# Thirty-two more tokens get their expert activations from gathered rows instead of the dense product

## The reference, cut to what matters

```python
s1, s2 = einsum(q1, keys1), einsum(q2, keys2)        # 8 heads x 128 keys each
v1, i1 = top_k(s1, 16); v2, i2 = top_k(s2, 16)
top_s, top_c = top_k(v1[..., :, None] + v2[..., None, :], 16)
expert = e1 * 128 + e2                                # 128 slots per token
g = softmax(top_s)
act = gelu(einsum('thkd,td->thk', u_tab[expert], h))
y = einsum('thk,thkd->td', g * act, v_tab[expert])
```

## Time and profile before

| | |
|---|---|
| median of 3 runs | 1529.41 us (1522.24 to 1529.96) |
| profiled execution | 1525.89 us, span 1524.1 us |
| PE busy | 1492.7 us (98%) |
| DVE busy | 1204.3 us (79%) |
| ACT busy | 703.4 us (46%) |
| POOL busy | 1021.8 us (67%) |
| moved by DMA | 439.99 MB, mean 289 GB/s |
| granted TensorE clock, mean | 0.992 |

### The profile page before, as it was taken

The page is one execution under the profiler, slowest core; times in us unless marked ns, Lnnn a source line. Parts: engine busy times, 40 slices in busy tenths (PEclk is TensorE's granted clock), DMA queues, the critical chain, the costliest instruction groups (busy, mean ns, idle before and its releaser), DMA issues.

```text
span 1524.1 us, 21845 instructions
## 1 busy us (share of the span) xinstructions
PE 1492.7 (98%) x7979; PEld 1253.3 (82%) x7979; DVE 1204.3 (79%) x1979; ACT 703.4 (46%) x1312; POOL 1021.8 (67%) x622
## 2 busy tenths in 40 slices
PE   7999999899999999999999999999999999999997
PEld 4345684488899999999999999988888888788885
DVE  6878833526799899998888880288999899999998
ACT  2034653342344433488888883433333333333343
POOL 2621002654378888776777875698888888889866
PEclk8999999999999999999999999999999999999999
DMA  9986137133178898889999997799999999999981
GB/s 364 338 242 100 26 103 284 43 123 111 45 268 323 312 334 306 298 294 374 361 376 362 384 352 295 262 375 346 374 388 379 383 387 381 375 382 370 368 288 69
DMA packets 216599, 439.99 MB, mean 289 GB/s; under 512 B 38180, under 2 KB 128804, under 8 KB 214572
## 3 DMA queue, kind: packets, MB, share of 16 engines
q1 hardware_dynamic: 178764, 303.49, 57.0%
q0 software_dynamic: 36864, 134.23, 23.8%
q10 hardware_dynamic: 864, 0.86, 0.2%
HBM read 380.72 MB, written 56.64 MB: 287 GB/s over the span
## 4 chain that ended last, share of the span: by engine, by line
PE 61%; DMA 9%; DVE 7%; issue 7%; POOL 4%; ACT 2%; SPq 2%; DVEq 0%; ACTq 0%
PE ps L1846 12%; PE ps L1848 11%; PE ps L1847 11%; DMA a_in<-act_scr 4%; DMA v_raw<-in_peer_v 4%; PE ps L1869 3%; PE ps L1871 3%; PE ps L1870 3%; POOL vl L1737 3%; DVE ps L1941 2%; PE ps L1515 2%; PE ps L1516 2%; PE ps L1517 2%; PE ps L1861 1%; PE ps L1862 1%
## 5 line engine op out<-in xcount | busy, mean ns | idle before, releaser
L1731 POOL TENSOR_TENSOR utl<-u_raw,uth 128x1024 fp32r<-128x1024 f32 x128 | 312.8, 2444 | 139.1 <-ACT uth L1750 120.8
L1846 PE MATMUL ps<-h2h,uth 128*128 128x384 f32 x1024 | 347.8, 340 | 2.2 <-POOL utl L1731 1.5
L1737 POOL TENSOR_TENSOR vl<-v_raw,vh 128x1024 fp32r<-128x1024 f32 x128 | 309.8, 2421 | 50.9 <-ACT vh L1750 48.9
L1848 PE MATMUL ps<-h2h,utl 128*128 128x384 f32 x1024 | 342.8, 335 | 0.0
L1847 PE MATMUL ps<-h2l,uth 128*128 128x384 f32 x1024 | 342.6, 335 | 0.0
L1869 PE MATMUL ps<-vh,wh 128*128 128x512 f32 x768 | 299.7, 390 | 0.8 <-DVE wl L2067 0.7
L1871 PE MATMUL ps<-vh,wl 128*128 128x512 f32 x768 | 299.2, 390 | 0.0
L1870 PE MATMUL ps<-vl,wh 128*128 128x512 f32 x768 | 299.1, 390 | 0.0
L2062 DVE TENSOR_TENSOR w_f<-a_in,g_in 128x384 f32<-128x384 f32 x128 | 213.8, 1671 | 94.6 <-DMA a_in<-act_scr 93.5
L1750 ACT ACTIVATE vh<-v_raw 128x1024 fp32r<-128x1024 f32 x128 | 135.4, 1058 | 194.7 <-DMA v_raw<-in_peer_v 163.5
L1846 PEld LDWEIGHTS ps<-h2h,uth 128*128 128x128 f32 x1024 | 192.4, 188 | 2.7 <-POOL utl L1731 1.8
(11 more groups left out here) (375 smaller groups left out, 2235.1 us busy)
## 6 DMA issues: line engine op xcount, KB each, us to landing
u_raw<-in_peer_uT SPq DMA_DIRECT2D x128, 512.0 KB, 7.0
v_raw<-in_peer_v SPq DMA_DIRECT2D x128, 512.0 KB, 9.3
act_scr<-acts SPq DMA_DIRECT2D x64, 384.0 KB, 4.7
g_scr<-stage SPq DMA_DIRECT2D x12, 2048.0 KB, 9.6
g_in<-g_scr SPq DMA_DIRECT2D x32, 768.0 KB, 8.7
a_in<-act_scr SPq DMA_DIRECT2D x64, 384.0 KB, 9.3
w_ada<-in_w_ada SPq DMA_DIRECT2D x10, 2048.0 KB, 15.8
w_q<-in_peer_w_query SPq DMA_DIRECT2D x8, 1024.0 KB, 6.4
```

Of the source, the lines that this page charges most:

```text
L1731: tt(k.utl[b % 3][:, :, :].rearrange(f3), k.u_raw[:, b % 4].rearrange(f3), k.uth[b % 3][:, :, :].bitcast(F32).rearrange(f3), ALU.subtract) ...
L1737: tt(k.vl[:, n % 4], k.v_raw[:, n % 4], k.vh[:, n % 4].bitcast(F32), ALU.subtract).then_inc(k.vl_done, 1)
L1846: mm(o, hi, k.h2h[:, kt, SP:T], start=(kt == 0), stop=False)
L1848: ins = mm(o, lo, k.h2h[:, kt, SP:T], start=False, stop=(kt == DK - 1))
```

## The change

The dense tile shrinks from 384 to 352 columns in the u stage: tokens 128 to 159 (SPX = 32) are left out of the activation product. Their activations are made from gathered u rows as for the special tile. As there are only 32 of them, the 128 partitions hold four groups (GX): group g has all 32 tokens and a quarter of the slots (SLX = 32). So 32 more gathers suffice, 160 u rows in all. Their h is made from `x1_scr` and two rows of `mod_scr` (six DMAs, two operations on POOL at block 3). The indices are spread to the groups, and the dot products collected, by four small DMAs each. The columns of `acts` of these tokens are filled with ones once; gate x activation goes into the one-hot weights instead (`special_weights`), scaled by each token's largest value, and ACT undoes the scale in `evacuate_g` for the first 8 groups. The one-hot blocks move from 57..113 to 63..118. Rows are issued and used at other places: the first behind block 16, and 12 u rows are used in v blocks 1 to 6.

```diff
-HOT_FROM, HOT_TO = 57, 113
+HOT_FROM, HOT_TO = 63, 118
+SPX = 32
+GX = P // SPX
+SLX = SLOTS // GX
+U_ROWS = SLX + SLOTS
+ONES_PAST = SP + SPX
@@ row_steps
-    for j in range(2 * SLOTS):
-        if j < 53:
-            at = 7 + 0.86 * j
-        elif j < 125:
-            at = 53 + (j - 53) * 0.777
-        elif j < SLOTS:
-            at = 109 + (j - 125) * 0.5
-        else:
-            at = NBLK + 1 + (j - SLOTS) * 0.875
+    for j in range(U_ROWS + SLOTS):
+        if j < 47:
+            at = max(16.9 + 0.755 * j, 10.7 + 0.93 * j)
+        elif j < 131:
+            at = 55.5 + (j - 47) * 0.72
+        elif j < U_ROWS:
+            at = 116 + (j - 131) * 0.65
+        else:
+            at = NBLK + 7 + (j - U_ROWS) * 0.78
@@ experts
-    SP_GELU, SP_WEIGH = 4, 6
+    SP_GELU, SP_WEIGH = 9, 11
+    INDICES_AT, GELX_AT = 15, 45
@@ sync
+        def load_special_rows():
+            sp.wait_ge(k.q_evac, k.items_all)
+            sp.wait_ge(k.s_x1out, 16 * TT)
+            for g in range(GX):
+                sp.dma_start(k.hx[g * SPX:(g + 1) * SPX, :], k.x1_scr[SP:SP + SPX, :]).then_inc(s_hx, 16)
+            for dst, row in ((k.ring[6], k.mod_scr[1, 0:2]), (k.ring[7], k.mod_scr[0, 2:4])):
+                row = row.rearrange("g n -> (g n)")
+                sp.dma_start(dst[:, :], bass.AP(row.tensor, row.offset, [[0, P], [1, D]])).then_inc(s_hx, 16)
+
+        def spread_indices():
+            sp.wait_ge(k.spx_done, 1)
+            for g in range(GX):
+                sp.dma_start(k.rowx_at[g * SPX:(g + 1) * SPX, :], k.spx_at[0:SPX, g * SLX:(g + 1) * SLX]).then_inc(s_spx, 16)
+
+        def spread_scales():
+            sp.wait_ge(k.spx_done, 2)
+            sp.dma_start(k.spx_scr, k.sx[0:SPX, 1:2]).then_inc(s_spx, 16)
+            sp.wait_ge(s_spx, 16 * (2 * GX + 1))
+            sp.dma_start(k.sbx[:, :], bass.AP(k.spx_scr.tensor, k.spx_scr.offset, [[0, P], [1, SPX]])).then_inc(s_spx, 16)
+
+        load_special_rows()
         for b in range(NBLK):
             if b + 4 < NBLK:
                 load_u(b + 4)
+            if b == INDICES_AT:
+                spread_indices()
+            elif b == GELX_AT + 1:
+                collect_activations()
+            elif b == HOT_FROM - 1:
+                spread_scales()
@@ gpsimd
+            if b == 3:
+                pool.wait_ge(s_hx, 16 * (GX + 2))
+                k.pool_steps.on(pool)(tt(k.hx[:, :], k.hx[:, :], k.ring[6][:, :], ALU.mult))
+                tt(k.hx[:, :], k.hx[:, :], k.ring[7][:, :], ALU.add).then_inc(k.hx_ready, 1)
@@ scalar
-            nc.scalar.activation(k.acts[:, b % 4], ps[:, 2 + b % 2, 0:TD], ACT.Gelu_apprx_tanh).then_inc(k.gelu_done, 1)
+            nc.scalar.activation(k.acts[:, b % 4, SPX:], ps[:, 2 + b % 2, 0:T - ONES_PAST], ACT.Gelu_apprx_tanh).then_inc(k.gelu_done, 1)
+
+        def finish_special():
+            act.wait_ge(k.row_used, SLX)
+            copy(y_sp, k.h_row[:, :]).then_inc(k.h_sp, 1)
+            nc.scalar.activation(k.dotsx[:, :], k.dotsx[:, :], ACT.Gelu_apprx_tanh).then_inc(k.gelx_done, 1)
@@ evacuate_g
+            if n < SPX // HOTS:
+                act.wait_ge(s_spx, 16 * (2 * GX + 2))
+                for j in range(HOTS):
+                    ins = nc.scalar.activation(k.stage[:, ch % 2, :, at + j], ps[:, 4 + n % 2, j * PKEYS:(j + 1) * PKEYS], ACT.Copy,
+                                               scale=k.sbx[:, HOTS * n + j:HOTS * n + j + 1])
+                ins.then_inc(k.g_evac, 1)
+                return
-        EXP_AT = {5: 0, 12: 1, 29: 2, 48: 3}
+        EXP_AT = {6: 0, 13: 1, 32: 2, 53: 3}
@@ tensor, activations
-                mm(o, hi, k.h2h[:, kt, SP:T], start=(kt == 0), stop=False)
-                mm(o, hi, k.h2l[:, kt, SP:T], start=False, stop=False)
-                ins = mm(o, lo, k.h2h[:, kt, SP:T], start=False, stop=(kt == DK - 1))
+                mm(o, hi, k.h2h[:, kt, ONES_PAST:T], start=(kt == 0), stop=False)
+                mm(o, hi, k.h2l[:, kt, ONES_PAST:T], start=False, stop=False)
+                ins = mm(o, lo, k.h2h[:, kt, ONES_PAST:T], start=False, stop=(kt == DK - 1))
@@ vector
-        routing(1, (3, 3))
-        for it, rows in ((2, (5, 5, 5, 2, 4, 4)), (3, (5, 5, 4, 2, 3, 3))):
+        routing(1, (0, 0))
+        special_indices()
+        for it, rows in (((2, (5, 5, 5, 2, 4, 4)), (3, (5, 2, 6, 3, 3, 3)))):
             for j in range(4):
                 topk(it, j)
                 use_rows(rows[j])
             routing(it, rows[4:])
+        special_weights()
@@
         for m in range(NBATCH):
             hots(m)
-            use_rows(3)
-        use_rows(SLOTS - done["rows"])
+            use_rows(3 + m % 2)
+        use_rows(U_ROWS - 12 - done["rows"])
 
         weight(0)
         for n in range(1, NBLK):
             weight(n)
             split_w_low(n - 1)
+            if n < SP_GELU and done["rows"] < U_ROWS:
+                use_rows(2)
@@
-                use_rows(min(SLOTS, (n - SP_WEIGH + 1) * 8 // 7) + SLOTS - done["rows"])
+                use_rows(min(SLOTS, (n - SP_WEIGH + 1) * 5 // 4) + U_ROWS - done["rows"])
```

66 lines of the change are left out of this document (54 added, 12 removed).

## The result

The changed kernel takes 1604.93 us (median of 4 runs, 1597.44 to 1607.38), the kernel before 1526.12 us in the runs beside it (4 runs, 1522.24 to 1529.96). The ratio is 1.052, with an interval of 1.049 to 1.055. The prediction said 1518 us, in a range of 1500 to 1538. The profiled execution took 1604.18 us, of which the span is 1602.3: 78.2 us more than before.

A forecast was written before the change was run, and what follows sets the result against it. PE's matmul pace was taken to bound both stages, with DMA also near its limit. Terms -41 + 3 + 0 + 9 + 2 + 9 + 7 = -11 us gave 1515 us profiled, 1518 us as median, range 1500 to 1538.

The forecast's parts named there:

- Routing, 0: Before the one-hot blocks: DVE finishes its routing and row 32 in time, costing 0 us, upper bound 6 us.
- One-hot blocks and the tail, +9: Blocks 61 to 127: DMA must move 123.3 MB, at 394 GB/s taking 313 us against PE's 304, +9 us.
- The joint, +9: Between u and v stages: late rows delay w(3), wh(3) and gelu(127), so PE waits in v block 0, +9 us.
- v blocks, +7: v stage: denser rows raise DMA need to 398 GB/s against some 390, costing 7 us.
- Start, +3: Start of the u stage: hx loads and two POOL operations delay utl of block 3, +3 us, bounds 0 and 8.
- -41 for the shorter matmul: u stage: 3072 matmuls lose 32 columns each, 13.3 ns apiece, -41 us where nothing else sets the pace.
- Scales, +2: First 8 groups: ACT's four small evacuations replace one, +2 us; SP's store wait of some 3 us stays hidden.
- slower rival: Both stages: DMA ceiling is 378 GB/s, u stage and v blocks lose 22 us each, 1546 us; chance 0.18.
- DMA follows PE: Both stages: DMA runs at 406 and 398 GB/s and PE keeps its pace, 1502 us; chance 0.22.
- DVE falls behind in the routing: Block 45 or an EXP_AT block: ACT waits 6 to 15 us for DVE, 1524 to 1533 us; chance 0.15.

The follow-up runs named there:

- row pace alone: Changed kernel with u rows 47 to 130 issued from block 58.5, one per 0.66 blocks, instead of from 55.5, one per 0.72: 1587.64 us.
- three rows a batch: Changed kernel with 3 instead of 3.5 rows per 16-token batch, fetches re-spaced, 12 rows moved into blocks 114 to 127: 1597.68 us.
- 56 blocks: Changed kernel with rows issued from block 58.5 per 0.66 blocks, and one-hot blocks 63 to 119 instead of 63 to 118: 1584.28 us.
- loosening: Changed kernel with the last 12 u rows used in v blocks 4 to 9 instead of 1 to 6: 1600.53 us.
- narrow kernel: Kernel before with only the 352-column matmuls and ones in acts, no rows gathered for tokens 128 to 159: median 1498.25 us, ratio 0.983.
- half the dots: Changed kernel with rows issued from block 58.5 per 0.66 blocks, DVE's dot products from row 47 over 512 of 1024 elements: 1589.65 us.

## Why the prediction was wrong

**The failed step is "Routing, 0", with what it left out.** I asked whether DVE has row 32 by block 45 (it had: gelu(45) to gelu(47) are undisturbed) and whether the routing is done by block 61, and took the row issues as mere work on POOL, 0.96 us each. I didn't ask where in POOL's queue an issue finds its buffer in use. My own numbers would have shown it: row 55 is put behind block 61.3, 8 rows behind row 47, and row 47 is used only behind the first batch, which needs the products that PE makes at block 61. In its place the runs showed a wait of 12.6 us of POOL on the ring, 10.4 us of PE idle behind it and some 3 us more at the halved clock, in four blocks that took 12.5 us more than before where I had 4 less. The row pace alone gave 17 us back, but not where the gap was: 3.9 us came back in these four blocks, since the wait for the scales came out behind it, 10.3 from gelu(64) to gelu(112), 5.4 in the tail and 2.2 in the v stage, less 5 us by which this execution was later at gelu(60). So this step is the one that failed by its mechanism, and it is not the whole miss. Of the 89 us between the forecast of -11 and the measured 78.2, 56 lie from gelu(60) to the first v matmul, 26 in the v stage and 7 between gelu(0) and gelu(60).

**One-hot blocks and the tail, +9: mis-sized, and by the wrong mechanism in the first part.** From gelu(60) to the first v matmul the differences add up to +47.2 us where my terms gave -9, 56 us off with the turn in it. I made the sum of the bytes, 406 GB/s, against a ceiling and stopped there. For gelu(64) to gelu(112) that bound doesn't hold: 341 GB/s at a share of 0.92, and half the rows' bytes give 1.4 us back. For the last blocks (965 to 1023 us, 404 GB/s, share 1.03) it does in part: SP stood 10.69 us in one issue of a_in, ACT waited up to 5.3 us for u_raw, and half the rows' bytes bring gelu(120) to gelu(125) from 25.6 to 20.5 us, but the whole tail only from 69.3 to 65.6. The row pace helped both parts; three rows a batch and 56 blocks shortened the first and lengthened the second.

**The joint, +9: right** in place and chain, and in size for the gap (9.2 us). The 3.4 us that v blocks 0 to 3 lose beyond it are the clock at 0.50 around the gap, which was in no term. That loosening gave 12.7 us back matches by chance in part: 7.2 of them came from these blocks.

**v blocks, +7: the mechanism right, the size not.** 29.5 us of gaps. I took a ceiling of 390 GB/s between 402 and 378; the window has 380, within 2 of the rival's figure, and +22 was the rival's price. The bare 402 row, nothing but weights streaming in, was no guide for a mix with a_in, g_in and gathers; the nearest row was the v stage's own, at a share of 1.04. The Trainium skill, HBM Reference, Specifications (TRN2), says that a core streaming alone gets more than its share of some 358 GB/s, about 425; by that the v stage's 398 GB/s would have fitted. The traces agree that more than the share is moved (404 and 380 GB/s); they differ as to 425, since the DMA share stood above 1 at 380, and they decide.

**Start, +3: mis-sized.** 6.9 us, within its bounds of 0 to 8. The data for POOL came later than the 414 us estimated (415.45), PE wanted utl of block 3 at 417.0 us and not at 418.8, and the clock at 0.50 behind the gap, in no term, made 5.6 us of waiting into 6.9. The whole stretch to gelu(60) lost some 7 us against my terms, 4 of them here; the rest is in small gaps and in the pace of the matmuls, below.

**-41 for the shorter matmul: right as a pace, wrong as a gain.** Alone it brings 27 us, with one wait at a fixed place of ACT's queue as the largest single loss. In the changed kernel it is worth 10.

**Scales, +2: the work over-priced, the wait under-priced.** The small evacuations cost nothing measurable. But I took SP's wait for the short store as some 3 us and harmless. It takes 7.1 us, and ACT then waits for the scales 1.3 us in the changed kernel and 4.0 to 4.9 us in the versions whose row pace is mended. What it is worth wasn't measured: every version of the changed kernel keeps it.

**The rivals.** The slower rival was right for the v stage and wrong for the one-hot blocks; it got the sign and fell 59 us short, since the turn, the queue order and the lowered clock of TensorE were in no rival. "DMA follows PE" and "DVE falls behind in the routing" fell: DVE was indeed ready some 16 us later than before (652.1 against 636.0), but with that mended by 8 us the turn cost the same.

**Open.** With the row pace and 56 blocks mended the stretch from gelu(64) to the first v matmul takes 318.1 us, the narrow kernel's 284.4 (284.4 is 957.9 - 673.5). Half the rows' bytes give 5 us of it and half the dots 3. Whether the rest, some 25 us, comes from the later place of the blocks or from more rows in the same queues wasn't parted. It wasn't tried to give fewer tokens to the gathered rows.

## What to carry to other kernels

An asynchronous load into a ring is a wait as soon as it is issued more than a ring's length ahead of its use: write for each issue what frees its buffer, and look at what stands behind it in the same queue, above all when it feeds the engine that bounds the kernel. Match the issue rate to the use rate, and time its start by the first use. When one wait is mended, look for what stood hidden behind it: here the scales, behind the ring. When a DMA stage is already at a share above 1, price added bytes at that stage's own rate, and treat work saved on the busiest engine as a gain only after asking which fixed place of another queue it will now reach too early: the 41 us were 27 alone and 10 in the changed kernel.

## What the runs showed of the hardware

The granted clock falls with the wait: PE did nothing from about 659 to 669 us and came back at 0.50 (1.2 GHz), its matmuls 0.29 us apart, and was at 1.00 again from about 675 us on; the window from 674 to 678 us, with both levels in it, has 0.83 in the mean. The mean over the kernel is 0.972 (before 0.992). From 669.3 to 674 us that is 2.3 us lost and in the next window another 0.7: a gap of 10 us costs some 3 us more than itself. It adds up. From gelu(60) to the first v matmul the gaps of PE over 0.3 us sum to 42 us in the changed kernel, and its matmuls at the lower clock lose some 17 us more; with the row pace mended it is 28 and 9.

The pace of the same matmul isn't one number. From 546 to 576 us, first the changed kernel, then the narrow one:

```profile
546.00:576.00 30.00, 30.00 (x182) 30.00 (x181) 29.38 (x74) 11.40 (x16) 25.70 (x18) 1.00 0.99 357
```

```profile
546.00:576.00 30.00, 30.00 (x192) 30.00 (x191) 29.38 (x136) 11.10 (x16) 27.29 (x18) 1.00 0.97 353
```

Both have 352 columns, a granted clock of 1.00, and no gap, but 164.8 and 156.3 ns for each matmul. The slower pace comes in whole stretches (blocks of 4.0 in place of 3.8 us, blocks 31 to 41 in the changed kernel) and costs about 0.2 us a block. What sets it wasn't found. The Trainium skill, TensorE: Matmul & The Clock Gate (Wait — 56ns, not 53.3ns?), gives N columns / 2.4 GHz and 2.5 ns more from one matmul to the next, an estimate of 149.2 ns for 352. Both windows are above it, by 7 and by 16 ns, and the rule has one pace at that clock where the trace has two.
